# Hybrid GLA / sparse-attention / mLSTM trunk: summing the mLSTM weights on TensorE instead of VectorE, and a decay projection without row halves

## What is computed

```python
g = log_sigmoid(a_lr @ w_gla_a2 + b_gla_a) / GLA_TAU     # (T, 16) @ (16, 512)
```

```python
P   = exp(D - m[..., None]) * einsum("bhtk,bhsk->bhts", q, k)
num = w_inter * (q @ C) + einsum("bhts,bhsv->bhtv", P, v)
den = w_inter * (q . n) + sum(P, axis=-1)
h   = num / maximum(abs(den), exp(-m))
```

## Time and profile before

| | |
|---|---|
| median of three runs | 1272.39 us |
| the profiled execution's own time | 1271.54 us |
| its span, first to last instruction | 1269.8 us |
| TensorE matmul busy | 1261.8 us |
| VectorE, ScalarE, GpSimd busy | 620.7, 393.8, 774.9 us |
| mean granted TensorE clock | 0.999 of full speed |

### The profile page before, as it was taken

The page is one execution under the profiler, slowest core; times in us unless marked ns, Lnnn a source line. Parts: engine busy times, 40 slices in busy tenths (PEclk is TensorE's granted clock), DMA queues, the critical chain, the costliest instruction groups (busy, mean ns, idle before and its releaser), DMA issues.

```text
span 1269.8 us, 17601 instructions
## 1 busy us (share of the span) xinstructions
PE 1261.8 (99%) x6644; PEld 1036.7 (82%) x6644; DVE 620.7 (49%) x1105; ACT 393.8 (31%) x810; POOL 774.9 (61%) x919
## 2 busy tenths in 40 slices
PE   9999999999999999999999999999999999999998
PEld 8866887676899899887898887887888888888886
DVE  4258788652266877834446663342511111333434
ACT  5243565543013334234033333311510111221322
POOL 8737430034764754747875546785776767888882
PEclk9999999999999999999999999999999999999999
DMA  7755200222322312222342323522233333222221
GB/s 188 229 168 169 72 17 26 63 72 77 100 67 67 84 50 67 67 83 69 114 108 81 96 85 110 186 98 86 74 110 85 98 98 102 100 92 91 100 83 67
DMA packets 168476, 120.63 MB, mean 95 GB/s; under 512 B 12409, under 2 KB 146655, under 8 KB 168392
## 3 DMA queue, kind: packets, MB, share of 16 engines
q1 hardware_dynamic: 161654, 108.32, 29.3%
q10 hardware_dynamic: 6738, 11.18, 2.7%
HBM read 115.23 MB, written 9.62 MB: 98 GB/s over the span
## 4 chain that ended last, share of the span: by engine, by line
PE 99%; DVE 0%; ACT 0%; issue 0%; DVEq 0%; ACTq 0%
PE GP L1840 46%; PE GP L1876 9%; PE PA L1876 9%; PE GP L1855 7%; PE GP L1837 7%; PE PA L2040 3%; PE GP L2102 3%; PE PA L2139 2%; PE PA L2077 1%; PE PA L2253 1%; PE GP L2328 1%; PE GP L1921 1%; PE PA L2010 1%; PE PA L2245 1%; PE PA L2041 1%; PE GP L1847 1%
## 5 line engine op out<-in xcount | busy, mean ns | idle before, releaser
L623 POOL TENSOR_TENSOR wlo<-wraw,whi 128x256 fp32r<-128x256 f32 x712 | 565.6, 826 | 14.8
L619 POOL TENSOR_SCALAR whi<-wraw 128x1024 fp32r<-128x1024 f32 x178 | 202.3, 1136 | 455.8 <-PE GP L1840 224.7
L1840 PE MATMUL GP<-xh,whi 128*128 128x512 f32 x352 | 145.6, 414 | 0.0
L1840 PE MATMUL GP<-xh,wlo 128*128 128x512 f32 x352 | 139.1, 395 | 0.0
L1840 PE MATMUL GP<-xl,whi 128*128 128x512 f32 x352 | 138.8, 394 | 0.0
L1782 DVE TENSOR_TENSOR ul<-U,uh 128x512 fp32r<-128x512 f32 x64 | 65.0, 1050 | 109.7 <-ACT uh L1147 109.7
L1840 PE MATMUL GP<-nh,whi 128*128 128x512 f32 x240 | 95.1, 396 | 0.0
L1840 PE MATMUL GP<-nl,whi 128*128 128x512 f32 x240 | 95.1, 396 | 0.0
L1840 PE MATMUL GP<-nh,wlo 128*128 128x512 f32 x240 | 95.1, 396 | 0.0
L1786 DVE SCALAR_TENSOR_TENSOR U<-GP,rrow 128x512 f32<-128x512 f32 x32 | 22.1, 691 | 141.7 <-PE GP L1840 140.3
L1840 PEld LDWEIGHTS GP<-xh,whi 128*128 128x128 f32 x352 | 66.3, 188 | 16.4 <-issue 2.0
(11 more groups left out here) (416 smaller groups left out, 2788.9 us busy)
## 6 DMA issues: line engine op xcount, KB each, us to landing
wraw<-in_w_in SPq DMA_DIRECT2D x75, 512.0 KB, 3.8
wraw<-in_w_up SPq DMA_DIRECT2D x32, 512.0 KB, 4.0
wraw<-in_w_down SPq DMA_DIRECT2D x32, 512.0 KB, 3.5
line_rows<-bias_line SPq DMA_DIRECT2D x8, 655.0 KB, 5.4
table<-line_rows SPq DMA_DIRECT2D x4, 1024.0 KB, 5.1
wraw<-in_w_br_dsa SPq DMA_DIRECT2D x8, 512.0 KB, 4.0
wraw<-in_w_br_gla SPq DMA_DIRECT2D x8, 512.0 KB, 4.0
wraw<-in_w_br_ml SPq DMA_DIRECT2D x8, 512.0 KB, 4.0
```

The lines of the kernel that those rows point to most:

```text
L619: nc.gpsimd.tensor_scalar(hi, src, 1.0, 1.0, ALU.mult, ALU.mult).then_inc(hi_done, 1)
L623: part = nc.gpsimd.tensor_tensor(lo[:, at:to], src[:, at:to], hi[:, at:to].bitcast(FP32), ALU.subtract)
L1840: ins = mm(ps[0:t.m, 0:SEQ], wt[:, s0, w], av, start=st, stop=sp_)
```

## The change

Three edits. The mLSTM sums are made by a third call of `recalled` with ones in the place of the values, and by `ones16`, ones on the 16 meta rows and zeros below, for the last 16 columns; `weight_sums` and its semaphore go, and two fills make `ones16`. The decay projection uses all 128 partitions of `a2` and `small`, with `a2` zero outside partitions 32 to 47; the second load of `a2` and the copy in `small` go, and the wait for the load stands ahead of `gq0`. The fill of `M` is waited for where `M` is read, and no longer right behind the fill.

```diff
@@ region BO
+    ("ones16", [P, P], FP32)
@@ ScalarE
-            for r in (2 * META, 0):
-                act.dma_start(a2[r:r + META, :], a["w_gla_a2"][0]).then_inc(ld_a, 16)
+            act.dma_start(a2[32:32 + META, :], a["w_gla_a2"][0]).then_inc(ld_a, 16)
@@ VectorE
             dve.wait_ge(gla_c, 1)
-            nc.vector.tensor_copy(small[0:2 * META, HALF:ALL], small[2 * META:4 * META, HALF:ALL]).then_inc(gla_c, 1)
-            dve.wait_ge(ld_a, 48)
+            dve.wait_ge(ld_a, 32)
...
-                    seq(nc.vector.memset(M_[GR, :], 1.0))
+                    nc.vector.memset(M_[GR, :], 1.0).then_inc(M_one, 1)
...
+                    dve.wait_ge(M_one, 1)
                     seq(nc.vector.tensor_tensor_scan(bcum, M, lf, 0.0, ALU.mult, ALU.add))
...
-                    nc.vector.memset(later[:, :], 0.0).then_inc(ml_c, 1)
+                    nc.vector.memset(later[:, :], 0.0)
+                    nc.vector.memset(ones16[:, :], 0.0).then_inc(ml_c, 1)
                     dve.wait_ge(ml_c, 1)
+                    nc.vector.memset(ones16[0:META, :], 1.0).then_inc(ml_c, 1)
...
-            def weight_sums(h):
-                dve.wait_ge(at_ok, 5 * h + 5)
-                t = Wd[:, 0, :]
-                seq(tt(t[:, FROM[1]:SEQ], AT[:, 0, FROM[1]:SEQ], AT[:, 1, 0:SEQ - FROM[1]], ALU.add))
-                for j in (2, 3):
-                    seq(tt(t[:, FROM[j]:SEQ], t[:, FROM[j]:SEQ], AT[:, j, 0:SEQ - FROM[j]], ALU.add))
-                t = t[0:META, SEQ - META:SEQ]
-                tt(t, t, ATt[0:META, :], ALU.add).then_inc(sum_w, 1)
...
-                weight_sums(h)
@@ TensorE
-                        r = slice(2 * META * (1 - b), 2 * META * (2 - b))
-                        ins = mm(ps[:, b * SEQ:b * SEQ + HALF], a2[r, h * DK:(h + 1) * DK], small[r, b * HALF:(b + 1) * HALF],
+                        ins = mm(ps[:, b * SEQ:b * SEQ + HALF], a2[:, h * DK:(h + 1) * DK], small[:, b * HALF:(b + 1) * HALF],
...
+            pe.wait_ge(ld_a, 32)
-            gemm("gq0")
-            gemm("gk0")
-            pe.wait_ge(ld_a, 48)
-            pe.wait_ge(gla_c, 2)
-            for nm in ("gg0", "gv0A", "gv0B", "gv0M"):
+            for nm in ("gq0", "gk0", "gg0", "gv0A", "gv0B", "gv0M"):
                 gemm(nm)
...
-                mm(bank(3)[:, 0:FROM[1]], ones[:, :], AT[:, 0, 0:FROM[1]], start=True, stop=True)
-                pe.wait_ge(sum_w, h + 1)
-                mm(bank(3)[:, FROM[1]:SEQ], ones[:, :], Wd[:, 0, FROM[1]:SEQ], start=True, stop=True).then_inc(av_ps, 1)
+                recalled(bank(3), lambda j: ones[:, :], ones16[:, :]).then_inc(av_ps, 1)
```

More of the change, by code:

```diff
@@ L383, in build @@
             ("gch", [P, ALL], FP32)])
-        (zc, cv, sgc, lf_, bcum_, M_, uT, uTt, fbias_, um_, Mb, Md, Wd, Mt, Wt, ATt, later_t) = region(BO, [
+        (zc, cv, sgc, lf_, bcum_, M_, uT, uTt, fbias_, um_, Mb, Md, Wd, Mt, Wt, ATt, later_t, ones16) = region(BO, [
             ("zc", [P, ALL + 3], FP32), ("cv", [P, ALL], FP32), ("sgc", [P, ALL], FP32), ("lf", [P, ALL], FP32),
@@ L390, in build @@
             ("Mt", [2 * META, META], FP32), ("Wt", [2 * META, META], FP32), ("ATt", [P, META], FP32),
-            ("later_t", [2 * META, META], FP32)])
+            ("later_t", [2 * META, META], FP32), ("ones16", [P, P], FP32)])
         later = ATm
@@ L479, in build @@
         xt_ok, ml_c = sem("xt_ok"), sem("ml_consts")
-        ms_ok, ms_d, sum_w = sem("ms_ok"), sem("ms_d"), sem("sum_w")
+        ms_ok, ms_d, M_one = sem("ms_ok"), sem("ms_d"), sem("M_one")
         ld_h, ld_g, tok_done, o_ss, h_ok, n_ok = sem("ld_h"), sem("ld_g"), sem("tok_done"), sem("o_ss"), sem("h_ok"), sem("n_ok")
@@ L1693, in _ @@
                 conv_mul(0, q)
-            dve.wait_ge(ml_c, 2)
+            dve.wait_ge(ml_c, 3)
             dve.wait_ge(ld_v, 16)
@@ L2265, in _ @@
                 if h == 0:
-                    pe.wait_ge(ml_c, 2)
+                    pe.wait_ge(ml_c, 3)
                 nxt("mq", 0)
```

## The result

The changed kernel took 1278.76 us (median of four runs, 1278.52 to 1279.53) against 1272.21 us before in the same rounds: a ratio of 1.0053, with an interval of 1.0039 to 1.0068. It is slower by 6.55 us; 1278.6 was predicted.

A forecast was written before the change was run, and what follows sets the result against it. TensorE's instruction stream was taken as the bound. Terms 5.88 (sums) + 0.39 + 0.05 (decay projection) - 0.1 (VectorE's relief) gave 6.2 us on a median of 1272.4, so 1278.6 us, 0.49% slower; range 1276.0 to 1280.8.

The forecast's parts named there:

- The bound: Whole kernel: TensorE, busy 1261.8 of 1269.8 us, sets the time; its waits stay under 3 us, busy time rises 6.
- The sums: 1.47 us a head: Four mLSTM heads: a third `recalled` call at 2.46 us replaces products of 0.99 us, 5.88 us in all.
- The gain from VectorE's relief: 0.1 us: mLSTM heads: projections beside VectorE's removed additions speed up, 0 to 0.44 us possible, 0.1 us taken in all.
- Its rival, 2.6 us: mLSTM heads: lighter VectorE speeds TensorE over whole heads, 0.65 us each, 2.6 in all, giving 1276.0 us; chance 0.05.
- The decay projection: 0.39 + 0.05 us: GLA heads: full-height group plus following level costs 0.13 us more in heads 1 to 3; head 0 at most 0.05.
- upper bound of 0.25 a head: Decay projection, GLA heads 1 to 3: group rises from 0.64 to 0.89 us with no gain in the level behind.
- the cover by `kh`: GLA head 0: next projection waits until 352.79 for VectorE's reading of `kh`, covering 0.89 of 0.93 us.
- The rest at nothing: Small pieces: earlier `a2` wait, dropped load and copy, two fills of 128 columns, `M`'s later wait; all cost nothing.
- The cover ahead of `yc0`: End of the branch: 2.30 us between VectorE's last low part and `yc0` exceeds the 1.47 us delay; no wait appears.
- The swallowed work: Behind the mLSTM heads: hidden TensorE waits for weight chunks absorb the added 5.9 us, giving 1272.8 us; chance 0.04.
- the new wait: Last mLSTM head: `yh` slips one projection, 5.6 us, making a 3.3 us wait, 1281.9 us; chance 0.06.

The follow-up runs named there:

- The two parts measured alone: Kernel before with only the mLSTM sums edit and M's wait: 1278.45 us, ratio 1.0051; with only the decay projection edit, its load and wait: 1272.87 us, ratio 1.0008.

## Why the prediction was right

**The bound.** TensorE's stream was the time, and its waits stayed under 3 us after, even with the sums made twice. Right. Its busy time rose by 8.4 us and not by 6, as much as the span of this one execution, with 1.07 us from the start.

**The sums: 1.47 us a head.** The third call took 2.33 + 0.13 us, as predicted from the second. Head to head it is 105.90/3 - 101.26/3 = 1.55 us, and 6.24 in all where I had 5.88. The step was right and the term 0.08 us a head too small: the projections behind the sums take 5.75 us and not 5.67. They now follow a product of 16 columns, and that seems to be the reason, as above.

**The gain from VectorE's relief: 0.1 us.** It doesn't exist. This is the one step that failed in kind. I compared two groups of 24 projections that differ in what precedes them as well as in what runs beside them, and picked the second; without the additions both kept their times. Its rival, 2.6 us, falls with it.

**The decay projection: 0.39 + 0.05 us.** It is 0.88 and nothing. The level behind the group fell from 0.82 to 0.65, a little further than the 0.70 that I drew between its neighbours. The group was the mis-sized term: 1.09 us between two levels, not the 0.89 of the row near the start, which stands between projections; the group of head 0, between projections too, has 0.89 on the chain. Of these 0.20 us, 0.11 lie at the group's beginning: its second record starts 0.33 us after the first between levels (379.41, 379.74) and 0.22 in head 0 (352.93, 353.15). The other 0.09 lie in where the chain cuts records that overlap. The upper bound of 0.25 a head was thereby just missed, by 0.02 for the group with its level.

In head 0 the last pair of records ahead of the group starts at 351.53 before and at 352.69 after, and the first projection behind it at 352.79 and 353.95, so 1.26 us in both. The group is 0.09 us longer (1.02 against 0.93) and starts 0.09 us sooner, and the cover by `kh` hid the rest. The other 0.12 of the 0.21 in the table lie in the projections behind, up to the second head. They belong to this one execution: the same stretch takes 24.80 us before and 24.92 after, but 24.81 both with the decay projection alone (353.63 to 378.44) and with the sums made twice (353.66 to 378.47).

**The rest at nothing.** The earlier wait, `M`'s fill and the fill of 128 columns are shown to cost nothing, to within about 1 us by the times and with no wait in the view. The copy in `small` that goes and the second fill of `ones16` had no run of their own; no wait appears where they stand. The cover ahead of `yc0` was 2.3 us after as well: the last low part ends at 814.21 + 1.84 = 816.05, `yc0` starts at 818.34.

```profile
814.21 1.84 DVE L1507 TENSOR_TENSOR yl<-on,yh 128x512 fp32r<-128x512 f32 x2 [7.98 <-ACT yh L911]
```

**The rivals.** The swallowed work was ruled out by the doubled sums, 9.7 of 9.84 us in the trace; the new wait did not appear even there.

**The sum.** By the traces the change costs 6.24 + 0.88 = 7.1 us, 6.2 were predicted and 6.55 measured between medians. The two parts measured alone give 6.69 + 1.11 = 7.8 with intervals of some 1.6 and 1.1 us to either side. The three terms that were off were off in the same direction, 0.36, 0.1 and 0.44 us, 0.9 in all. So the hit on 1278.6 within 0.2 us is partly luck: it owes the rest to the scatter of the start, about 1 us from run to run.

## What to carry to other kernels

Where TensorE has hardly a wait, additions that VectorE makes in its idle time are free, and each column moved from them onto TensorE is paid in full: 832 columns of fp32 a head cost 1.5 us here. Price such a column by the same shapes in the chain, and take the row whose neighbours are also the same, since what stands before and behind a group moved its time by 0.1 to 0.2 us. A gain on TensorE is another matter: taking 2.5 us out of the GLA heads gave 0.1 until VectorE's order was changed, so look at which engine is next, and by how little, before counting a saving.

## What the runs showed of the hardware

Two fp32 products of 32 rows and 264 columns between two levels take 0.64 us together on different bands and 1.08 on the same band, as much as at full height (1.09). A level of fp32 products with 96 stationary columns takes 0.65 us behind a full-height product and 0.82 behind one of 32 rows. A product of 512 columns with ones took 0.95 us as plain fp32 in its two records, and 0.33 + 0.23 us as two fp32r products of one record each. Removing 2.8 us of VectorE's additions a head left the projections beside them at 5.70 us. The three `conv` operations on VectorE took 2.38 us with GpSimd idle and 3.46 with GpSimd splitting beside them all along, while the splitting took 4.45 us instead of 3.85.
